# Decays inside a chunk from 32-row products of running sums instead of products over tables of steps

## What is computed

```python
a_cs = jnp.cumsum(dt * A, axis=2)                 # per chunk of 128, per head; A < 0
seg = a_cs[:, :, :, None] - a_cs[:, :, None, :]   # over pairs (l, s) of positions of a chunk
decay = jnp.exp(jnp.where(lower, seg, -jnp.inf))
cb = jnp.einsum("bclgn,bcsgn->bclsg", Cm, Bm)
y_diag = jnp.einsum("bclsgj,bcsgjp->bclgjp", cb[..., None] * decay, xdt)
```

## Time and profile before

| | |
|---|---|
| median of three runs | 3033.34 us |
| the profiled execution | 3033.2 us |
| its span, first to last instruction | 3031.9 us |
| PE busy | 2867.9 us, 95% of the span |
| DVE busy | 2249.0 us, 74% |
| ScalarE busy | 1271.5 us, 42% |
| GpSimd busy | 720.4 us, 24% |
| mean clock granted to TensorE | 0.981 |

### The profile page before, as it was taken

How to read it: one execution, slowest core, us unless ns; L and a number is a source line. 1 busy time by engine, 2 the same in 40 slices (tenths; PEclk the granted TensorE clock), 3 DMA queues, 4 the chain that set the end, 5 groups by cost and what they waited for, 6 DMA issues and landing times. The chain is left out here.

```text
span 3031.9 us, 39024 instructions
## 1 busy us (share of the span) xinstructions
PE 2867.9 (95%) x14496; PEld 2273.6 (75%) x14496; DVE 2249.0 (74%) x3445; ACT 1271.5 (42%) x2298; POOL 720.4 (24%) x561
## 2 busy tenths in 40 slices
PE   7999999999899999989899999999889999999999
PEld 6678876777688878867788777844567878887887
DVE  7355644599899964855998755889886767778888
ACT  2223331377678862223467576111364322223332
POOL 1032002355311110221134325010001143333221
PEclk9999999999899999999999999999999999999999
DMA  6345224544522316433137544231002233354331
GB/s 230 129 165 174 92 73 155 194 136 136 194 82 90 120 62 224 153 96 73 42 112 222 167 138 177 89 113 59 28 8 81 96 127 111 111 197 150 111 111 56
DMA packets 222333, 370.24 MB, mean 122 GB/s; under 512 B 19066, under 2 KB 120602, under 8 KB 222146
## 3 DMA queue, kind: packets, MB, share of 16 engines
q1 hardware_dynamic: 193378, 271.00, 27.3%
q0 software_dynamic: 28768, 96.76, 8.6%
HBM read 257.30 MB, written 109.08 MB: 121 GB/s over the span
## 5 line engine op out<-in xcount | busy, mean ns | idle before, releaser
L4589 PE MATMUL banks<-b3down_r_t 128*128 128x512 f32 x1344 | 307.4, 391 | 8.2 <-DVE b3down_r_t L4621 7.5
L4589 PEld LDWEIGHTS banks<-b3down_r_t 128*128 128x128 f32 x1344 | 253.6, 189 | 62.0 <-DVE b3down_r_t L4621 7.9
L837 PE MATMUL banks<-b_hThi,b1item_hi 128*128 128x512 f32 x464 | 194.8, 420 | 1.6 <-DVE b1ln_big L529 1.3
L4342 PE MATMUL banks<-b3up_t_t,b3up_w_w 128*128 128x512 f32 x768 | 182.9, 394 | 1.0 <-DVE b3up_w_w L4299 1.0
L2659 PE MATMUL banks<-b2h_hi,b2h_whi 128*128 128x512 f32 (+1 forms) x448 | 177.6, 396 | 4.8 <-DVE b2h_lo L2061 2.4
L837 PE MATMUL banks<-b_hThi,b1item_lo 128*128 128x512 f32 x464 | 181.7, 392 | 0.0
L837 PE MATMUL banks<-b_hTlo,b1item_hi 128*128 128x512 f32 x464 | 181.2, 391 | 0.0
L2659 PE MATMUL banks<-b2h_lo,b2h_whi 128*128 128x512 f32 (+1 forms) x448 | 176.0, 393 | 0.0
L2659 PE MATMUL banks<-b2h_hi,b2h_wlo 128*128 128x512 f32 (+1 forms) x448 | 176.0, 393 | 0.0
L4342 PEld LDWEIGHTS banks<-b3up_t_t,b3up_w_w 128*128 128x128 f32 x768 | 143.8, 188 | 36.1 <-DVE b3up_w_w L4299 2.5
L1757 DVE CUSTOM_DVE_ANT_0 b1att_map<-banks,b1att_dist 128x1024 f32<-128x1024 f32 x128 | 151.5, 1221 | 8.5 <-PE banks L1670 6.3
(11 more groups left out here) (614 smaller groups left out, 7496.7 us busy)
## 6 DMA issues: line engine op xcount, KB each, us to landing
b1raw_w<-in_w_in SPq DMA_DIRECT2D x32, 512.0 KB, 3.7
qk_spill<-b1scan_qk SPq DMA_DIRECT2D x64, 256.0 KB, 3.2
b1out_ws<-in_w_out SPq DMA_DIRECT2D x16, 1024.0 KB, 5.1
b3upr_raw<-in_w_mlp_up SPq DMA_DIRECT2D x16, 1024.0 KB, 5.2
b3down_a_t<-act_spill SPq DMA_DIRECT2D x16, 1024.0 KB, 6.1
b3down_b_t<-in_w_mlp_down SPq DMA_DIRECT2D x16, 1024.0 KB, 8.7
b2h_stage<-in_w_in SPq DMA_DIRECT2D x30, 512.0 KB, 4.0
b1item_stage<-in_w_in SPq DMA_DIRECT2D x29, 512.0 KB, 5.2
```

Of the source, the lines that this page charges most:

```text
L837: last = K.pe.matmul(pair[:, ss], a, b, start=q % 2 == 0 and i == 0, stop=q % 2 == 1 and i == 11)
L4342: last = pe.matmul(out, y[:, 4 * half + k], z[:, k], start=c == 0, stop=c == 11)
L4589: last = pe.matmul(K.bank[b], x[:, q, cols], y[:, q], start=c == 0, stop=c == 11)
```

## The change

The exponent of a pair of positions is now the difference of two running sums, taken by one product of 32 rows. For each direction and group, 32 partitions of `m.turned` hold the running sums of 8 heads as rows, high parts (8 rows) and low parts (8), and ones; `m.rhs` holds in the same 32 partitions minus the pick of each head, the running sums of the chunk as rows (2, loaded anew for each chunk), and again the pick. A product of the two gives, for 4 heads, sum at l less sum at s. The forward direction lands in one bank of `K.pair[1]`, the backward one in the other. On the wrong side of the diagonal a difference is positive and the right one negative, so the smaller of both is the wanted exponent: ScalarE copies the backward half to `m.X` (`backward_exponents`), DVE takes the minimum with the forward half in PSUM (`smaller`), ScalarE takes the exponential from `m.X`.

- PE: `tri` goes; `exponents(k)`, two products, is called four times a round, spread between the quarters, the first call at the end of the backward half. Each call waits for `smaller` of the one before.
- In the first backward round PE multiplies the steps with the masks once more, 16 small products (`turned_sums`), so that the sums lie by head. ScalarE and DVE split them (`turned_hi`, two copies; two subtractions), SP stores them (4) and loads them back in the third backward round (8 loads and 8 of rows).
- Rows for later chunks: four loads a round on SP, of 2 rows x 8 x 128, between `yb` and the item.
- ScalarE: `decays` goes (24 copies of 128x128 for a group); `forward_weights`, 8 such copies for a group, makes `Cf`.
- GpSimd: `weights` makes `Cb` and adds `Cf` to it, instead of making both.
- DVE: `both` and `lows` go; `smaller`, four a round, comes. At the start of the scan: 7 small sums for `pick`, two fills of `rhs` and one of `turned`, where two masks and `dtA_lo` were made.

The diff, cut:

```diff
@@ sp_scan
+    def cum_rows(c):
+        if c >= ST:
+            return
+        if c >= 2:
+            sp.wait_ge(S["sc_tri"], 4 * (c - 1))
+        for gr in range(GROUPS):
+            for d in range(2):
+                at = block_rows(d, gr).start + 16
+                L.start(sp, ("cum_row", c, d, gr), m.rhs[c % 2][at:at + 2].bitcast(F32), K.cum_dram[d, :, 8 * gr:8 * gr + 8, c * P:(c + 1) * P])
...
+        if r == 2:
+            turned_in()
+            cum_rows(0)
+            cum_rows(1)
+        if r > ST:
+            cum_rows(r - ST + 1)
+def block_rows(d, gr):
+    return slice(64 * d + 32 * gr, 64 * d + 32 * gr + 32)
@@ pe_scan
+    def turned_sums():
+        pe.wait_ge(S["conv_raw"], 12)
+        pe.wait_ge(S["conv_out"], 10)
+        for d, mask in enumerate((K.upper, K.lower)):
+            for c in range(ST):
+                last = pe.matmul(K.pair[1 + d][0:HEADS, c * P:(c + 1) * P], K.dtA[:, c, d * HEADS:(d + 1) * HEADS], mask, start=True, stop=True)
+            last.then_inc(S["cum_turned"], 1)
+    def exponents(k):
+        c, gr, half = k // 4, k // 2 % 2, k % 2
+        if k:
+            pe.wait_ge(S["sc_L"], k)
...
+            at = block_rows(d, gr)
+            last = pe.matmul(K.pair[1][:, d * 512:(d + 1) * 512], m.turned[at, c], m.rhs[c % 2][at, 4 * half:4 * half + 4], start=True, stop=True)
+        last.then_inc(S["sc_tri"], 1)
...
-            tri(c, 0)
             pe_quarters(K, QK_PLAN[ST + c][0])
+            exponents(4 * c + 2)
             if c:
                 carried(("off", c), c)
             pe_quarters(K, QK_PLAN[ST + c][1])
             inside(c, 0)
-            tri(c, 1)
+            exponents(4 * c + 3)
             if c < ST - 1:
                 gathered(("new", c), c, ST + c)
             pe_quarters(K, QK_PLAN[ST + c][2])
             if c < ST - 1:
                 cb(c + 1)
+                exponents(4 * c + 4)
             pe_quarters(K, QK_PLAN[ST + c][3])
+            if c < ST - 1:
+                exponents(4 * c + 5)
             inside(c, 1)
@@ act_scan
+        for j in range(8):
+            h = gr * 8 + j
+            last = a.activation(m.Cf[:, j], m.cb[gr][0], ACT.Copy, scale=K.dt[:, c, h:h + 1])
+        last.then_inc(S["sc_C"], 1)
...
+        to = m.X[:, 4 * half:4 * half + 4].rearrange("p h l -> p (h l)")
+        a.activation(to, K.pair[1][:, 512:1024], ACT.Copy).then_inc(S["sc_copied"], 1)
...
             exps(c, 0)
-            decays(c, 1, 0)
             act_quarters(K, QK_PLAN[ST + c][0])
+            backward_exponents(4 * c + 2)
             if c:
                 diagonal(c - 1)
-            decays(c, 1, 1)
+            forward_weights(c, 1)
             act_quarters(K, QK_PLAN[ST + c][1])
+            backward_exponents(4 * c + 3)
             exps(c, 1)
-            if c + 1 < ST:
-                decays(c + 1, 0, 0)
             act_quarters(K, QK_PLAN[ST + c][2])
             if c + 1 < ST:
-                decays(c + 1, 0, 1)
+                backward_exponents(4 * c + 4)
             act_quarters(K, QK_PLAN[ST + c][3])
+            if c + 1 < ST:
+                backward_exponents(4 * c + 5)
+                forward_weights(c + 1, 0)
@@ pool_scan
+        g.tensor_tensor(m.Cb, over(dt, 2, P), over(m.cb[gr][1], 1, 8), ALU.mult).then_inc(S["sc_back"], 1)
+        g.wait_ge(*S.at("sc_back", n + 1))
+        g.wait_ge(S["sc_C"], n + 1)
+        g.tensor_tensor(m.Cb, m.Cb, m.Cf, ALU.add).then_inc(S["sc_low"], 1)
@@ dve_scan
+    def smaller(k):
+        half = k % 2
+        v.wait_ge(*S.at("sc_copied", k + 1))
+        to = m.X[:, 4 * half:4 * half + 4].rearrange("p h l -> p (h l)")
+        v.tensor_tensor(to, to, K.pair[1][:, 0:512], ALU.min).then_inc(S["sc_L"], 1)
...
             dve_quarters(K, QK_PLAN[ST + c][0])
+            smaller(4 * c + 2)
...
-            lows(c, 1)
...
-            both(c, 1)
...
             inner(c, 0)
+            smaller(4 * c + 3)
...
                 masked(c + 1)
-                lows(c + 1, 0)
+                smaller(4 * c + 4)
             dve_quarters(K, QK_PLAN[ST + c][3])
             if c < ST - 1:
-                both(c + 1, 0)
+                smaller(4 * c + 5)
```

More of the change, by code:

```diff
@@ L1237, in gathered @@
         last.then_inc(S["sc_m"], 1)
+    def turned_sums():
[9 more added lines that the diff above has]
+            pe.wait_ge(S["sc_L"], k)
+        else:
+            pe.wait_ge(*S.at("cum_lo", 2))
+        for d in range(2):
+            if half == 0:
+                pe.wait_ge(*K.loads[("cum_row", c, d, gr)])
+                if c == 0:
+                    for part in range(2):
+                        pe.wait_ge(*K.loads[("cum_in", d, gr, part)])
+            at = block_rows(d, gr)
+            last = pe.matmul(K.pair[1][:, d * 512:(d + 1) * 512], m.turned[at, c], m.rhs[c % 2][at, 4 * half:4 * half + 4], start=True, stop=True)
+        last.then_inc(S["sc_tri"], 1)
     for b in range(ST):
@@ L1248, in pe_scan @@
             cb(0)
+            exponents(0)
         pe_quarters(K, QK_PLAN[b][2])
[L1251 to L1263, removed]
+    exponents(1)
     def inside(c, gr):
@@ L1338, in act_scan @@
     for b in range(ST):
[L1339 to L1342, removed]
         for place in range(3):
+            if b == 0 and place == 1:
+                turned_hi()
+            if b == ST - 1 and place == 2:
+                backward_exponents(0)
             act_quarters(K, QK_PLAN[b][place])
+    backward_exponents(1)
+    forward_weights(0, 0)
     a.wait_ge(S["lam_dot"], 2)
@@ L1396, in weights @@
             g.wait_ge(S["sc_M"], n)
[L1397 to L1399 removed]
+        else:
+            for d in range(2):
+                for part in range(2):
+                    g.wait_ge(*K.loads[("cum_out", d, part)])
+        dt = K.dt[:, c, 16 + gr * 8:16 + gr * 8 + 8]
+        g.tensor_tensor(m.Cb, over(dt, 2, P), over(m.cb[gr][1], 1, 8), ALU.mult).then_inc(S["sc_back"], 1)
+        g.wait_ge(*S.at("sc_back", n + 1))
+        g.wait_ge(S["sc_C"], n + 1)
+        g.tensor_tensor(m.Cb, m.Cb, m.Cf, ALU.add).then_inc(S["sc_low"], 1)
     for b in range(ST):
@@ L1520, in dve_scan @@
     v.wait_ge(*K.loads["eye"])
-    vs.mark(v.tensor_tensor(K.below, K.lower, K.eye, ALU.subtract))
-    vs.mark(v.tensor_tensor(K.above, K.upper, K.eye, ALU.subtract))
-    v.wait_ge(S["dtA_hi"], 1)
+    places = [K.eye[:, 32 * i + 8 * part:32 * i + 8 * part + 8] for i in range(4) for part in range(2)]
+    then(v.tensor_tensor(K.pick, places[0], places[1], ALU.add))
+    for place in places[2:]:
+        then(v.tensor_tensor(K.pick, K.pick, place, ALU.add))
+    for rhs in m.rhs:
+        vs.mark(v.tensor_scalar(rhs, over(K.pick, 2, P), -1.0, None, ALU.mult))
     v.wait_ge(vs.sem, vs.n)
-    v.tensor_tensor(K.dtA_lo, K.dtA, K.dtA_hi, ALU.subtract).then_inc(S["dtA_lo"], 1)
+    v.tensor_scalar(m.turned, over(K.ones, 1, ST), 1.0, None, ALU.mult).then_inc(S["scan_set"], 1)
     for b in range(ST):
@@ L1537, in dve_scan @@
             v.wait_ge(S["bs_yb"], b)
+        if b == 0:
+            for d in range(2):
+                v.wait_ge(S["cum_hi"], d + 1)
+                v.tensor_tensor(m.cumT[d][1], K.pair[1 + d][0:HEADS], m.cumT[d][0], ALU.subtract).then_inc(S["cum_lo"], 1)
         dve_quarters(K, QK_PLAN[b][1])
```

86 lines of the change are left out of this document (56 added, 30 removed).

## The result

The changed kernel takes **3038.75 us** (median of 20 runs, 3034.75 to 3045.23) against 3033.84 for the kernel before, run beside it (20 runs, 3028.42 to 3038.68). The ratio is 1.0016, 95% interval 1.0010 to 1.0022: slower by a sixth of a per cent, where 0.8% faster was forecast and 3023 was the range's upper end. The profiled execution has a span of 3036.1 us, 4.2 more than before.

What follows compares the result with a forecast made beforehand. PE and DVE were taken as both nearly full, DVE's late state sum making PE wait. Savings of 17.1 + 2.0 + 1.1 + 4.0 - 0.5 = 23.7 us from 3033.2 gave 3009.5, said as 3009; range 2996 to 3023.

Steps and rivals of the forecast that it cites:

- TensorE's work: Scan rounds: PE work 24.2 us, less 3.7 for tri, plus 2.4 for four calls at 0.6, gives 22.9.
- 20.6, 2.3 under PE. So the state wait goes: DVE in a scan round: 25.5 less 7.6 plus 2.7 us gives 20.6, so PE stops waiting for the state sum.
- GpSimd: nothing: GpSimd in the scan: one of two products becomes a sum, 1.9 to 2.9 us either way, so no change.
- Half a microsecond to spare: Row loads in a round: land by 3.8 us after inner; PE's third call comes 5.3 us after inside ends.
- inner follows inside by 1 us when DVE isn't behind: Row loads in a round: the 1 us gap assumed in finding half a microsecond to spare before PE's third call.
- Copy, weights, sum, product in a row: Round zero: this chain before the first inside adds waits of about 1.5 us, within a net 1.1 us saved.
- Final round: From 779.16 to attention's first product, 20.1 us: shorter ScalarE work and perhaps some clock save 4.0 us.
- part of the clock: Final round: the last inside took 3.65 us for 1.9 at the lower clock; part of that may go.
- Backward half: 16 small products, 3.5 us, covered by a wait of 5.0; DVE's additions mostly hidden; 0.5 us charged.
- The loads rule: Rival: collisions of 1.7 us or late rows make rounds of 25 us, 9 lost of 17; 3020 us; chance 0.17.
- a loop of 22.7 us: Rounds: chain from item load through ScalarE, GpSimd and DVE to the next issue, just under PE's 22.9; 0.3 allowed.
- absorbed: Rival: collisions and late rows both hit every round, 26.1 us; only the final round gains; 3029 us; chance 0.07.

Runs made afterwards that it cites:

- all_early: Changed kernel with row loads issued first, next chunk's forward weights ahead of the last qk copy, and round zero's weights and first exponential earlier: 3007.73 us.
- start_early: Changed kernel with only round zero altered: first forward weights and the exponential's table load ahead of the backward half's last query/key copy: 3031.33 us.
- the moves: Three reorderings on the changed kernel: row loads, next chunk's forward weights, and round zero's weights and exponential, each issued earlier; all together 3007.73 us.
- rows_early: Changed kernel with SP issuing the next chunk's row loads ahead of the zg and yb loads: 3024.32 us.
- weights_early: Changed kernel with ScalarE making the next chunk's forward weights ahead of the round's last query/key copy: 3021.85 us.
- chunk_first: `all_early` with the loads of x and item ahead of the stores of turned sums in the first backward round: 3007.41 us.

## Why the prediction was wrong

By its own steps:

- **TensorE's work, right.** 22.9 us a round forecast, 23.05 measured in the changed kernel, and 22.96 is the whole round in `all_early`. A call takes 0.63 where 0.6 was taken, made of the same two parts. The page "TensorEngine Tiling (Array Packing)" of the Trainium skill says that a change of tiling mode drains TensorE, with no price; the 0.40 of a call agrees with it.
- **"20.6, 2.3 under PE. So the state wait goes", the step that failed.** The list of operations was right and VectorE's busy time nearly (21.8), but I took the other rows of VectorE as they stood. The gated reductions went from 0.81 to 2.6 us (mean of the 14 up to 790 us), 3.6 us a round, while the fade fell from 2.9 to 1.9 and the product ahead of the reductions from 2.4 to 1.2. The state wait shrank from 0.87 to 0.83 only. Where an operation is slow because of another engine's, a change in that engine's timing moves the slowness; it doesn't remove it.
- **"GpSimd: nothing", the step behind it.** The sum takes 3.0 us on average (15 in 45.3 us), a little over the 1.9 to 2.9 taken; what undid the forecast is its start, which was not looked up. I wrote that the sum now waits for ScalarE's weights and then asked only what stands behind it in GpSimd's queue, not when ScalarE gets there. It stood in the earlier trace rows and in the diff: the last copy of the round waits for TensorE, and the weights were put behind it. In the kernel before both halves of the next tables stood ahead of that copy.
- **"Half a microsecond to spare" for the row loads.** The call waits 4.7 us in all in six rounds; in the round shown 1.05. Issue to use is 3.1 us (669.21 to 672.27), as bounded. What failed is "inner follows inside by 1 us when DVE isn't behind": inside ends near 664.7, and inner starts 3.4 us later.
- **The clock in the rounds, not in the sum at all.** In the rounds of 26.8 to 27.1 the granted clock is 0.94; by the stretches with products every 0.43 us some 20 us in rounds zero to five ran at half clock, and half of that, 10 us, is lost. I had priced the clock in the final round alone.
- **Round zero, 1.1 gained forecast, 4.2 lost.** "Copy, weights, sum, product in a row" was put at 1.5. ScalarE's row is longer:

```profile
601.70 1.05 ACT L820 ACTIVATE b1item_hi<-b1item_stage 128x1024 fp32r<-128x1024 f32 x1
602.65 0.59 ACT L1410 ACTIVATE b1scan_X<-banks 128x512 f32<-128x512 f32 x1
603.12 2.44 ACT L1396 ACTIVATE b1scan_Cf<-b1scan_cb,b1ssm_dt 128x128 f32<-128x128 f32 x8
605.58 1.28 ACT L1436 ACT_TABLE_LOAD   x1
```

  It ends in a table load of 1.28 us, which the trace of the kernel before had too. TensorE waits 3.0 us for the product of this chain and then runs 6.8 us at half clock. `start_early` shows that this chain makes the whole 6 us by which round zero is longer than there (40.84 against 34.60).
- **Round six, 2.0 forecast, 0.3 lost.** Its row loads are late as well (TensorE waits 1.18 us for them, its longest wait there); with the moves it takes 20.79, where 20.4 was forecast.
- **Final round, half.** 4.0 forecast, 2.0 found, 3.6 in `all_early`. The late weights are the difference: 18.08 here and 18.04 in `rows_early`, but 16.58 in `weights_early`. TensorE's longest wait there is 5.07 us, and it is no shorter with the moves (5.05):

```profile
796.57 3.65 PE L1334 MATMUL banks<-b1scan_xs,b1scan_E 128*128 128x64 f32 x16 [5.07 <-DVE b1scan_E L1586]
800.01 3.40 PE L1246 MATMUL banks<-b1scan_diag,b1scan_y 128*128 128x128 f32 x16
803.34 0.96 PE L1770 MATMUL banks<-b1att_k,b1att_q 64*128 64x512 f32 x6
```

  The "part of the clock" of the earlier trace rows did not come back: the last passes take 3.65 us as before.
- **Backward half, 0.5 forecast, 0.7 found**, and 2.3 ahead of its first state product. Those 2.3 are no cost of the change: with the same code up to there, that product starts at 501.02 here and at 497.25 in `rows_early`, ahead of the kernel before. The small products were covered, as said; the wait of the earlier trace rows went from 5.0 to 3.8 us, and the 0.7 are half-clock time behind it (4.9 of a stretch of 6.8 us, instead of 3.4). The stores do not make the wait: it is 3.43 us with the loads behind them (`all_early`) and ahead of them (`chunk_first`).

The loads rule was the nearest rival, with both its conditions true (late rows, collisions of some 2 us), but on the reductions and not on `scaled`, and priced at 3020 to 3029 because it left out the clock and round zero. With "absorbed" it had 0.24 of the chance; it should have had more, since the forecast itself allowed half a microsecond in a loop of 22.7 us. That the order of queues undid the gain, and not the new arithmetic, is shown by `all_early`: the forecast's sum was 23.7 us, its profiled span is 24.4 under that of the kernel before (26.5 by the medians). Rounds of 22.96 stand for the forecast 23.2.

What stays open: why the same wait of 3.43 us is followed by 0 or 6.8 us at half clock, and one of 4.96 by 3.4; and how `weights_early` and `rows_early`, each with one lateness left, divide their 24.2 us a round.

## What to carry to other kernels

When work moves to another engine, look up in the trace when that engine's queue reaches the new place, and what the instruction ahead of it waits for; the duration of the work is the smaller question. Put work whose input is ready ahead of an instruction that is paced by TensorE, above all where a third engine waits for it and shares a path with a fourth. Where TensorE fills nearly the whole round, price what its clock may lose behind each new wait as well: here that was some 10 us beside some 12 of waits in rounds zero to five.

## What the runs showed of the hardware

- A pair of 32-row products (rows in the two halves of the array, 512 columns) mostly starts within 4 ns and costs 0.23 us, as one. A call of one pair between full products costs 0.63, of two pairs 0.86, of two full-height products 0.48.
- VectorE's reduction over 128x512, with both operands in SBUF, takes 0.69 us alone and 2.4 to 3.2 beside GpSimd's products and sums of 128x1024; its minima with one operand in PSUM stayed at 0.68 in every run.
- A load of 8 KB took 3.1 us from issue to first use, no less than the 3.0 to landing of the 256 KB stores.
- At one and the same wait of 3.43 us the half-clock stretch at its end was 6.8 us in eight kernels and absent in one (`chunk_first`), each read in one execution.
